# Five gated FFNs that multiply the unnormalized residual and take 1/rms at the read-out, in a two-block kernel on one core

## The chip, the cores and the metric

One core of a Trainium2 chip runs the whole program. The metric is the device time of one execution in microseconds, the median of several executions. TensorE multiplies, VectorE and ScalarE work elementwise, GpSimd adds a little, and 16 DMA engines bring the weights.

## What is computed

The reference runs two transformer blocks of two layers each on 256 tokens of width 1024. Cut to what matters here:

```python
def rmsnorm(x, gain):
    xf = x.astype(jnp.float32)
    y = xf * lax.rsqrt(jnp.mean(xf * xf, axis=-1, keepdims=True) + NORM_EPS)
    return (y * gain.astype(jnp.float32)).astype(x.dtype)

def modulate(h, shift, scale):
    return h * (1.0 + scale) + shift

def swiglu(u, wg, wu, wd):
    return (jax.nn.silu(u @ wg) * (u @ wu)) @ wd
...
    u = modulate(rmsnorm(h, norm_ffn2[l]), mod[:, :, 6], mod[:, :, 7])
    h = h + 0.5 * (1.0 + mod[:, :, 8]) * swiglu(u, ffn2_wg[l], ffn2_wu[l], ffn2_wd[l])
```

The first block has in each layer an FFN, a mixer (retention, stick-breaking attention, a state space part) and a second FFN; the second block has a mixer of three attentions and one FFN per layer. That is six FFNs with an inner width of 2816. The modulation vectors come from products of a condition vector with large matrices (the "ada" matrices).

## The kernel before

Everything is held transposed: width on the 128 partitions (8 tiles, KT), the 256 tokens along the free dimension. Stages follow in the order `STAGES`: f1, m1, f2 for each layer of the first block, a final norm, then m2, f3 for each layer of the second block (`FFN` numbers the six FFNs 0 to 5).

**Split products.** Every float32 product is made as three fp32r matmuls of high and low halves (`mm3`, lines 706 to 709): high weight by high and by low activation, low weight by high activation, each with its own weight load of 128x128 and 256 moving columns. All matmuls through the helper `mm` stand in the profile as L704.

**Weights.** One stream in the order of use: `fill`s of 1 MB by DMA from SP's queue into a ring of three slots, each two "grains" of 128x1024. ScalarE makes each grain's high half (`split`, L1246), VectorE its low half (L1728), into four slots; a slot is free when TensorE has read the grain four before.

**One FFN** (`ffn` in each engine's program). For each of the 22 inner tiles (a unit: one gate grain, one up grain) TensorE makes 2 x 8 x 3 matmuls into the two halves of one of four banks. Unit 0 goes by k, gate and up together, waiting for each k of u; the others go grain by grain. ScalarE takes the silu of the gate half from the bank (L1355), VectorE multiplies it by the up half (L1847), ScalarE copies the high half of the result (L1361), VectorE makes the low half (L1853). Then the down product: 8 output tiles of 22 x 3 matmuls, 22 grains; VectorE adds each to h (L1832), ScalarE squares it (L1336), GpSimd adds the squares (L2239).

**The norm in front of an FFN** (`norm`). The squares of h are summed over partitions by TensorE with a matrix of ones (`sums`: two float32 matmuls after an FFN, eight otherwise), then 18 matmuls into an unused bank (`idle`). ScalarE makes 1/rms by Ln and Exp (L1267, L1270). For each of the 8 tiles VectorE makes h * gain * 1/rms (L1749), ScalarE adds the shift and rounds to the high half of u (L1284), VectorE makes the low half (L1755). Before it, behind a mixer, VectorE adds the last product to h (`residual`, L1822) and ScalarE squares it (L1263).

**Ada turns.** The ada matrices stream through a ring of their own, one 128x1024 piece a turn: ScalarE issues the DMA (L1234), VectorE makes the dot product (L1703). `RATE_IN`, `RATE_OUT` and `RATE_MIX` are the turns per grain in gate/up, down and mixers; a stage that needs a vector takes all turns up to it first.

Of the kernel before, what the change touches and what calls it, by code (L numbers as in the profile page):

```python
# [14 lines left out]
F32 = mybir.dt.float32  # L15
# [7 lines left out]
P = 128  # L23
D = 1024
# [404 lines left out]
RATE_IN, RATE_OUT, RATE_MIX = 0.36, 0.48, 0.52  # L429
# [24 lines left out]
class Memory:  # L454


    def __init__(self, nc, ctx):
# [12 lines left out]
        self.rope_t = self.sb("rope_t", 2 * 512)  # L470
# [24 lines left out]
        self.o_low = [self.sb(f"o_low{i}", 2 * T, F32R, base + 4 * at) for i, at in enumerate(O_LOW_AT)]  # L495
        self.hid_split = self.sb("hid", 2 * FT * T, F32R, base + 4 * HID_AT)
        self.psum = ctx.enter_context(nc.psum_tensor("bank", [P, 8 * 512], F32))
        self.banks = [self.psum[:, i * 512:(i + 1) * 512] for i in range(8)]
        self.hv = tiles(self.h, KT)
# [152 lines left out]

def gate_of(s):
# [14 lines left out]
def after_ffn(s):  # L668

    n = STAGES.index(s)  # L670
    return n > 0 and STAGES[n - 1] in FFN

# [27 lines left out]
def pe_program(pe, m):  # L700
# [140 lines left out]

    def ffn(s):
# [3 lines left out]
        for n in range(TOGETHER if f == 0 else 0, FT):  # L846
# [380 lines left out]
def act_program(act, m, dram):  # L1227
# [26 lines left out]

    def norm(s):
        gain, scale, shift = norm_of(m, s)
        if not after_ffn(s):
# [7 lines left out]
        act.wait_ge(("square_read", s, KT - 1))  # L1265
        b = m.banks[act.bank("norm", s)]
        act.e.activation(m.rs[:, 0:T], b[:, 0:T], ACT.Ln, scale=1.0 / D, bias=m.eps[:, 0:1]) \  # L1267
            .then_inc(*act.done(("out", "norm", s), ("mean_log", s)))
        act.wait_ge(("mean_log", s))
        act.e.activation(m.rs[:, 0:T], m.rs[:, 0:T], ACT.Exp, scale=-0.5).then_inc(*act.done(("rs", s)))  # L1270
# [55 lines left out]

    def ffn(s):
# [4 lines left out]
        def square(d):  # L1332
            act.wait_ge(("h", s, d))
            if d >= 4:
                act.wait_ge(("square_sum", follows, d - 3))
            act.e.activation(m.squares[:, square_slot(d), :], m.hv[:, d, :], ACT.Square) \  # L1336
                .then_inc(*act.done(("square", follows, d)))
            if follows == STAGES[-1]:
# [6 lines left out]
        for t in range(FT + 1):  # L1345
# [3 lines left out]
            if together:  # L1349
                split(first + wanted_first(t))  # L1350
            if t:
# [343 lines left out]
def dve_program(dve, m):  # L1695
# [55 lines left out]

    def low_of(s, d, shift):
# [26 lines left out]
    def norm(s):  # L1779
        gain, scale, shift = norm_of(m, s)  # L1780
        for job in (scale, shift):
            if job:
                ada(dve.ada.until(job))
        if scale:
            dve.wait_ge(("params",), ("mod", JOB[scale]))
            last = STAGES[STAGES.index(s) - 1]
            dve.wait_ge(("gained", KT - 1) if last == STAGES[0] else ("scaled", last, KT - 1))
# [29 lines left out]
    def residual(s):  # L1817
        gate = gate_values(s)
        for d in range(KT):
# [4 lines left out]
                .then_inc(*dve.done(*points))  # L1824

    def ffn(s):
        f = FFN[s]
        first = STREAM.index[first_grain(s)]

        def add(d):  # L1830
# [3 lines left out]
                .then_inc(*dve.done(("h", s, d), ("out", "acc", s, d)))  # L1834

        split(first + 2)
        for t in range(FT + 1):
            n = t - 1
            g = m.inner[n % 2]
            together = f == 0 and t <= TOGETHER  # L1840
# [376 lines left out]
def pool_program(pool, m):  # L2217
# [13 lines left out]
    def squares(s):  # L2231

        pool.wait_ge(("square", s, 0))
        for d in range(1, KT - 1):
# [68 lines left out]
    for s in STAGES:  # L2303
        if after_ffn(s):
            squares(s)
# [239 lines left out]
```

## Time and profile before

| | us |
|---|---|
| median of 3 runs | 2032.94 (2025.23 to 2040.07) |
| the profiled execution | 2031.49 |
| its span | 2029.5 |
| TensorE busy | 1947.2 |
| VectorE busy | 1469.0 |
| ScalarE busy | 1041.2 |
| GpSimd busy | 140.3 |

The span runs from the first to the last instruction of the profiled execution, which took 2.0 us more. Busy times of different engines lie beside one another. The profile names PE (TensorE), PEld (its weight loads), DVE (VectorE), ACT (ScalarE), POOL (GpSimd) and SP (the queue that issues the weight stream).

### The profile page before, as it was taken

How to read it: one execution, taken by the hardware profiler on the slowest of the kernel's cores; microseconds unless marked ns; L12 is line 12 of the kernel's file. 1: busy time of each engine (PE TensorE's matmuls, PEld its weight loads, DVE VectorE, ACT ScalarE, POOL GpSimd, SP SyncE). 2: the span in 40 equal slices, each digit the busy share in tenths (PEclk: the TensorE clock that was granted, in tenths of full speed). 3: DMA queues.
4: the chain of work that ended last, by engine and by line, in shares of the span. 5: the costliest groups of instructions: out<-in, count | busy, mean ns of one | idle time of the engine just before them, and what ended most of it. 6: DMA issues, size and time to landing. Idle time of an engine off the chain costs nothing.

```text
span 2029.5 us, 38168 instructions
## 1 busy us (share of the span) xinstructions
PE 1947.2 (96%) x16020; PEld 1901.1 (94%) x16020; DVE 1469.0 (72%) x2244; ACT 1041.2 (51%) x1623; POOL 140.3 (7%) x130
## 2 busy tenths in 40 slices
PE   6999999999999999999999989998999899999998
PEld 6999899899999999999899989898999899989998
DVE  6777877776767777878766767778767778776553
ACT  4554655455545545564544455464554455545453
POOL 3100012100000000022000010001000100010000
PEclk9999999999999999999999999999999999999999
DMA  9678664567777785655577845466677655544552
GB/s 369 252 271 318 243 236 169 218 224 264 274 249 257 266 294 216 240 186 208 218 254 251 294 170 198 179 220 230 217 265 282 240 205 206 190 156 164 190 204 104
DMA packets 83835, 466.39 MB, mean 230 GB/s; under 512 B 9424, under 2 KB 9552, under 8 KB 44496
## 3 DMA queue, kind: packets, MB, share of 16 engines
q1 hardware_dynamic: 48544, 334.98, 45.6%
q10 hardware_dynamic: 35120, 128.99, 17.8%
q8 instruction: 125, 2.05, 0.4%
q14 instruction: 46, 0.38, 0.1%
HBM read 462.88 MB, written 1.05 MB: 229 GB/s over the span
## 4 chain that ended last, share of the span: by engine, by line
PE 72%; DVE 12%; ACT 4%; issue 2%; POOL 1%; DVEq 0%; ACTq 0%
PE bank L704 71%; DVE low L1728 4%; DVE ada_ring L1703 2%; ACT high L1246 1%; DVE tmp L1749 1%; DVE u_split L1755 1%; PE bank L1047 1%; DVE region L1887 0%; ACT u_split L1284 0%; DVE region L2133 0%; POOL region L2269 0%; DVE region L2184 0%; ACT rs L1267 0%; ACT rs L1270 0%; DVE region L1697 0%
## 5 line engine op out<-in xcount | busy, mean ns | idle before, releaser
L704 PE MATMUL bank<-u_split,high 128*128 128x256 f32 x6464 | 1137.5, 281 | 26.3 <-DVE u_split L1755 17.4
L704 PEld LDWEIGHTS bank<-u_split,high 128*128 128x128 f32 x6464 | 982.8, 188 | 37.9 <-DVE u_split L1755 18.9
L1728 DVE TENSOR_TENSOR low<-ring,high 128x1024 fp32r<-128x1024 f32 x616 | 751.2, 1233 | 355.7 <-issue 226.4
L704 PE MATMUL bank<-u_split,low 128*128 128x256 f32 x3232 | 899.2, 278 | 0.0
L1246 ACT ACTIVATE high<-ring 128x1024 fp32r<-128x1024 f32 x616 | 617.2, 1046 | 86.8 <-PE bank L704 78.3
L704 PEld LDWEIGHTS bank<-u_split,low 128*128 128x128 f32 x3232 | 607.5, 188 | 0.4
L704 PE MATMUL bank<-hid,high 128*128 128x256 f32 x2112 | 363.4, 277 | 0.7 <-DVE low L1728 0.7
L704 PEld LDWEIGHTS bank<-hid,high 128*128 128x128 f32 x2112 | 319.2, 188 | 0.9 <-DVE low L1728 0.9
L1703 DVE SCALAR_TENSOR_TENSOR ada_ring<-ada_ring,cond 128x1024 f32<-128x1024 f32 x242 | 300.5, 1242 | 2.8 <-DMA ada_ring<-ada 2.8
L704 PE MATMUL bank<-hid,low 128*128 128x256 f32 x1056 | 292.6, 277 | 0.0
L704 PEld LDWEIGHTS bank<-hid,low 128*128 128x128 f32 x1056 | 198.2, 188 | 0.0
L1355 ACT ACTIVATE sil<-bank 128x256 f32<-128x256 f32 x132 | 50.9, 385 | 232.3 <-PE bank L704 232.2
L1361 ACT ACTIVATE hid<-sil 128x256 fp32r<-128x256 f32 x132 | 55.3, 419 | 98.8 <-DVE sil L1847 98.8
L2239 POOL TENSOR_TENSOR tmp<-tmp 128x256 f32<-128x256 f32 x36 | 26.6, 739 | 1127.5 <-ACT tmp L1336 1127.5
L1336 ACT ACTIVATE tmp<-h 128x256 f32<-128x256 f32 x48 | 20.1, 418 | 145.7 <-DVE h L1832 145.7
L704 PE MATMUL bank<-region 128*128 128x256 f32 (+2 forms) x312 | 70.7, 352 | 6.4 <-DVE xa L1868 4.7
L704 PE MATMUL bank<-high,u_split 128*128 128x256 f32 (+1 forms) x384 | 68.4, 279 | 2.1 <-DVE low L1728 2.1
L704 PEld LDWEIGHTS bank<-region 128*128 128x128 f32 (+1 forms) x312 | 53.7, 190 | 15.6 <-DVE xa L1868 5.5
L1749 DVE SCALAR_TENSOR_TENSOR tmp<-h,gcol,rs 128x256 f32<-128x256 f32 x80 | 41.4, 534 | 31.9 <-ACT rs L1270 31.9
L704 PEld LDWEIGHTS bank<-high,u_split 128*128 128x128 f32 x384 | 58.9, 188 | 2.5 <-ACT region L1393 1.4
L1853 DVE TENSOR_TENSOR hid<-sil,hid 128x256 fp32r<-128x256 f32 x132 | 55.5, 420 | 6.8 <-ACT hid L1361 6.8
L704 PE MATMUL bank<-merged,high 128*128 128x256 f32 x256 | 48.0, 292 | 11.8 <-DVE merged L2188 8.3
(213 smaller groups left out, 1823.6 us busy)
## 6 DMA issues: line engine op xcount, KB each, us to landing
ring<-stream SPq DMA_DIRECT2D x302, 1024.0 KB, 5.5
ada_ring<-ada ACTq DMA_DIRECT2D x240, 512.0 KB, 4.2
region<-ada SPq DMA_DIRECT2D x6, 1024.0 KB, 12.7
ring<-stream SPq DMA_DIRECT2D x4, 640.0 KB, 4.4
region<-na_bias ACTq DMA_DIRECT2D x2, 1024.0 KB, 4.8
ring<-stream SPq DMA_DIRECT2D x4, 512.0 KB, 3.9
cst<-const SPq DMA_DIRECT2D x1, 1600.0 KB, 8.9
cond<-cond SPq DMA_DIRECT2D x2, 512.0 KB, 5.5
```

Of the source, the lines that this page charges most:

```text
L704: return pe.e.matmul(out, lhs, rhs, start=start, stop=stop, skip_group_check=True)
L1047: t = pe.e.transpose(b[:, k * T + a * P:k * T + (a + 1) * P], m.S[p][:, a * T + k * P:a * T + (k + 1) * P], m.c2("ident"))
L1246: act.e.activation(hi, src, ACT.Copy).then_inc(*act.done(("high", n)))
L1336: act.e.activation(m.squares[:, square_slot(d), :], m.hv[:, d, :], ACT.Square) \
L1355: act.e.activation(g, m.banks[act.bank("hid", f, n)][:, 0:T], ACT.Silu).then_inc(*act.done(("silu", f, n)))
L1361: act.e.activation(m.hid[0][:, n, :], g, ACT.Copy).then_inc(*act.done(("hid_high", f, n)))
L1703: dve.e.scalar_tensor_tensor(out=w, in0=w, scalar=1.0, in1=m.cond[:, block * D:(block + 1) * D], op0=ALU.mult, op1=ALU.mult, accum_out=m.s ...
L1728: dve.e.tensor_tensor(lo, src, hi.bitcast(F32), ALU.subtract).then_inc(*dve.done(("low", n)))
L1749: dve.e.scalar_tensor_tensor(out=out, in0=m.hv[:, d, :], scalar=gain[:, d:d + 1], in1=m.rs[:, 0:T], op0=ALU.mult, op1=ALU.mult).then_inc(* ...
L1755: dve.e.scalar_tensor_tensor(out=m.ul[:, d, :], in0=src, scalar=m.mod(shift)[:, d:d + 1], in1=m.uh[:, d, :].bitcast(F32), op0=ALU.add, op1 ...
L1853: dve.e.tensor_tensor(m.hid[1][:, n, :], g, m.hid[0][:, n, :].bitcast(F32), ALU.subtract) \
L2239: pool.e.tensor_tensor(total, total, m.squares[:, square_slot(d), :], ALU.add) \
```

## The change

The five FFNs 1 to 5 (all but the first) no longer build u. ScalarE and VectorE make v = h * gain * (1 + scale), split in two, in a tile of 320-column rows, with the shift in two more columns behind the 256 of h. TensorE multiplies 258 columns, gate and up into a bank each (`ffn_linear`), so columns 256 and 257 hold the shift's product. At the read-out VectorE multiplies both banks, 2 x 258 columns, by [1/rms, 1, 1] into `scaled_out`; ScalarE takes the silu with column 256 as its bias; VectorE adds the up half's column 256 and multiplies. The sum of the squares stands on TensorE between gate and up of unit 1, and ScalarE makes 1/rms (`root`) there. v is made inside the residual loop behind a mixer, and in the down stretch behind an FFN. GpSimd adds the squares at all five. The idle matmuls and the norm of these stages are gone. There are no ada turns in the first four units of these FFNs, and RATE_OUT is 0.64 for 0.48.

```diff
-RATE_IN, RATE_OUT, RATE_MIX = 0.36, 0.48, 0.52
+RATE_IN, RATE_OUT, RATE_MIX = 0.36, 0.64, 0.52
...
+LINEAR = [("f2", 0), ("f1", 1), ("f2", 1), ("f3", 0), ("f3", 1)]
+UNITS, UNITS_QUIET = FT, 4
+TE = T + 2
+V_AFTER = {3: (0, 1), 4: (2, 3), 5: (4, 5), 6: (6,)}
...
     def norm(s):
+        if s in LINEAR:
+            return
         sums(s)
         idle(s)
 
     def sums(s):
-        b = banks.take("work", "norm", s)
-        if after_ffn(s):
+        b = banks.open(7, "norm", s) if s in LINEAR else banks.take("work", "norm", s)
+        if pooled(s):
...
+    def ffn_linear(s):
+        f = FFN[s]
+        for n in range(UNITS):
+            bs = [banks.open((2 * n + i) % 8, "hid", f, n, i) for i in range(2)]
+            if n == 0:
+                gs = [grain("gate", f, n), grain("up", f, n)]
+                pe.wait_ge(("v_shift", s))
+                for k in range(KT):
+                    pe.wait_ge(("v", s, k))
+                    for i in range(2):
+                        t = mm3(bs[i][:, 0:TE], [x[:, k, :] for x in gs[i][1]], (m.vh[k], m.vl[k]), k == 0, k == KT - 1)
...
+                if n == 1 and i == 0:
+                    sums(s)
...
+    def v_high(s, d):
+        act.wait_ge(("gcol", s), before(s)[d])
+        act.e.activation(m.vh[d][:, 0:T], m.hv[:, d, :], ACT.Identity, scale=m.gcol[:, d:d + 1]) \
+            .then_inc(*act.done(("v_high", s, d)))
+    def prepare(s):
+        act.e.preload_act_table_set(LOG_EXP)
+        first = STREAM.index[first_grain(s)]
+        shift_columns(s)
+        for d in range(KT):
+            v_high(s, d)
+            if d >= 4:
+                act.wait_ge(("square_sum", s, d - 3))
+            act.e.activation(m.squares[:, square_slot(d), :], m.hv[:, d, :], ACT.Square).then_inc(*act.done(("square", s, d)))
+            if d == 5:
+                split(first + 3)
...
+        if t == 1:
+            root(s)
+        if t:
+            act.wait_ge(("scaled_out", f, n))
...
+            act.e.activation(g, m.scaled_out[n % 2][:, 0, 0:T], ACT.Silu, bias=m.scaled_out[n % 2][:, 0, T:T + 1]) \
+                .then_inc(*act.done(("silu", f, n)))
+        split(upto + 4)
...
+    def v_low(s, d):
+        dve.wait_ge(("v_high", s, d))
+        dve.e.scalar_tensor_tensor(out=m.vl[d][:, 0:T], in0=m.hv[:, d, :], scalar=m.gcol[:, d:d + 1],
+                                   in1=m.vh[d][:, 0:T].bitcast(F32), op0=ALU.mult, op1=ALU.subtract) \
+            .then_inc(*dve.done(("v", s, d)))
...
+                dve.wait_ge(("full", "hid", f, n), ("rs", s), ("rs_tail", s))
+                dve.e.tensor_tensor(m.scaled_out[n % 2], two(m.psum[:, i * 512:(i + 2) * 512])[:, :, 0:TE],
+                                    spread(m.rs[:, 0:TE], 2), ALU.mult) \
+                    .then_inc(*dve.done(("scaled_out", f, n), ("out", "hid", f, n, 0), ("out", "hid", f, n, 1)))
+                split(upto + 3)
+                dve.wait_ge(("silu", f, n))
+                dve.e.scalar_tensor_tensor(out=g, in0=m.scaled_out[n % 2][:, 1, 0:T], scalar=m.scaled_out[n % 2][:, 1, T:T + 1],
+                                           in1=g, op0=ALU.add, op1=ALU.mult).then_inc(*dve.done(("prod", f, n)))
+            split(upto + 4)
```

VectorE behind the first mixer, before: eight residuals (h), then the gain columns, then pairs of normalized tile (tmp) and low half (u_split).

```order
L1809 TENSOR_SCALAR gates<-mods 128x8
L1822 SCALAR_TENSOR_TENSOR h<-bank,gates,h 128x256 x8
L1788 SCALAR_TENSOR_TENSOR gcol<-mods,par 128x8
L1749 SCALAR_TENSOR_TENSOR tmp<-h,gcol,rs 128x256 x2
L1755 SCALAR_TENSOR_TENSOR u_split<-tmp,mods,u_split 128x256
```

The same place with the change:

```order
L1954 TENSOR_SCALAR gates<-mods 128x8
L1877 SCALAR_TENSOR_TENSOR gcol<-mods,par 128x8
L1970 SCALAR_TENSOR_TENSOR h<-bank,gates,h 128x256
L1884 TENSOR_TENSOR v<-mods,v 128x8x2
L1970 SCALAR_TENSOR_TENSOR h<-bank,gates,h 128x256
L1890 SCALAR_TENSOR_TENSOR v<-h,gcol,v 128x256
```

The low half of v now follows each residual, one tile behind; nothing of u is left.

VectorE in one later unit of the same FFN, before (low are weights, sil the product, hid the low half, ada_ring a turn):

```order
L1728 TENSOR_TENSOR low<-ring,high 128x1024
L1847 TENSOR_TENSOR sil<-sil,bank 128x256
L1728 TENSOR_TENSOR low<-ring,high 128x1024
L1853 TENSOR_TENSOR hid<-sil,hid 128x256
L1703 SCALAR_TENSOR_TENSOR ada_ring,sums<-ada_ring,cond 128x1024
```

and with the change:

```order
L2012 TENSOR_TENSOR rope_t<-bank,rs 128x516
L1846 TENSOR_TENSOR low<-ring,high 128x1024
L2017 SCALAR_TENSOR_TENSOR sil<-rope_t,sil 128x256
L1846 TENSOR_TENSOR low<-ring,high 128x1024
L2022 TENSOR_TENSOR hid<-sil,hid 128x256
L1821 SCALAR_TENSOR_TENSOR ada_ring,sums<-ada_ring,cond 128x1024
```

One pass out of the banks (rope_t is where `scaled_out` lies) stands ahead of the first weight split; the rest keeps its order.

## Rows read from the trace of the kernel before

**Rows 1.** The page: busy time by engine, share of the span, instructions.
```profile
PE 1947.2 (96%) x16020; PEld 1901.1 (94%) x16020; DVE 1469.0 (72%) x2244; ACT 1041.2 (51%) x1623; POOL 140.3 (7%) x130
```

**Rows 2.** The chain in order of time: start, length, engine, tile, line, count.
```profile
423.61 174.42 PE bank L704 x1536
```

**Rows 3.** Stretches: length, busy time (instructions) by engine, granted clock, DMA.
```profile
410.10:416.50 6.40, 5.88 (x36) 5.22 (x35) 3.81 (x11) 4.49 (x11) 0.00 (x0) 1.00 0.39 160
423.60:538.10 114.50, 114.50 (x1010) 114.50 (x1011) 83.07 (x118) 57.61 (x85) 0.00 (x0) 1.00 0.75 265
538.10:598.00 59.90, 59.90 (x530) 59.90 (x529) 41.87 (x55) 27.05 (x32) 4.42 (x6) 1.00 0.82 286
976.10:982.70 6.60, 3.73 (x23) 3.56 (x22) 6.57 (x10) 3.66 (x4) 0.00 (x0) 0.82 0.70 240
```

**Rows 4.** Timeline, TensorE: start, length, instruction, count [idle before, releaser].
```profile
410.12 3.70 PE L704 MATMUL bank<-tmp,ones 128*128 128x256 f32 x16
...
413.48 2.50 PE L704 MATMUL bank<-high 128*128 128x256 f32 x18
...
416.52 0.47 PE L704 MATMUL bank<-u_split,high 128*128 128x256 f32 x2 [0.54 <-DVE u_split L1755]
...
423.61 0.50 PE L704 MATMUL bank<-u_split,high 128*128 128x256 f32 x2 [0.74 <-DVE low L1728]
...
597.85 0.59 PE L704 MATMUL bank<-tmp,ones 128*128 128x256 f32 x2
...
609.51 0.51 PE L704 MATMUL bank<-u_split,high 128*128 128x256 f32 x2 [0.75 <-DVE low L1728]
...
999.86 0.50 PE L704 MATMUL bank<-u_split,high 128*128 128x256 f32 x2 [0.75 <-DVE low L1728]
...
1432.17 0.50 PE L704 MATMUL bank<-u_split,high 128*128 128x256 f32 x2 [0.74 <-DVE low L1728]
...
1845.70 0.50 PE L704 MATMUL bank<-u_split,high 128*128 128x256 f32 x2 [0.78 <-DVE low L1728]
```

**Rows 5.** Timeline: residuals on VectorE behind the four mixers; squares on ScalarE.
```profile
409.12 3.23 DVE L1822 SCALAR_TENSOR_TENSOR h<-bank,gates,h 128x256 f32<-128x256 f32 x8
...
409.63 3.16 ACT L1263 ACTIVATE tmp<-h 128x256 f32<-128x256 f32 x8 [2.38 <-DVE h L1822]
...
982.66 0.88 DVE L1822 SCALAR_TENSOR_TENSOR h<-bank,gates,h 128x256 f32<-128x256 f32 x2
...
1416.42 3.44 DVE L1822 SCALAR_TENSOR_TENSOR h<-bank,mods,h 128x256 f32<-128x256 f32 x8
...
1829.08 1.65 DVE L1822 SCALAR_TENSOR_TENSOR h<-bank,mods,h 128x256 f32<-128x256 f32 x4
```

**Rows 6.** Groups by form, VectorE and ScalarE: busy us, mean ns, idle before.
```profile
L1728 DVE TENSOR_TENSOR low<-ring,high 128x1024 fp32r<-128x1024 f32 x608 | 746.4, 1241 | 355.7 <-issue 226.4 <-ACT high L1246 128.2
...
L1755 DVE SCALAR_TENSOR_TENSOR u_split<-tmp,mods,u_split 128x256 fp32r<-128x256 f32 x72 | 34.6, 481 | 3.3 <-ACT u_split L1284 3.3
...
L1697 DVE COPY region<-bank 128x512 f32<-128x512 f32 x10 | 6.9, 687 | 1.5 <-PE bank L704 1.5
...
L1246 ACT ACTIVATE high<-ring 128x1024 fp32r<-128x1024 f32 x608 | 613.1, 1052 | 86.8 <-PE bank L704 78.3 <-DVE ada_ring L1703 6.9 <-DMA ring<-stream 1.1
...
L1318 ACT ACTIVATE full<-h,gcol 128x256 f32<-128x256 f32 x8 | 4.0, 505 | 0.2
```

**Rows 7.** Timeline, VectorE, one unit of the second layer's first FFN.
```profile
643.90 1.22 DVE L1728 TENSOR_TENSOR low<-ring,high 128x1024 fp32r<-128x1024 f32 x1 [1.27 <-issue]
...
646.84 1.22 DVE L1703 SCALAR_TENSOR_TENSOR ada_ring<-ada_ring,cond 128x1024 f32<-128x1024 f32 x1
...
649.34 1.23 DVE L1728 TENSOR_TENSOR low<-ring,high 128x1024 fp32r<-128x1024 f32 x1 [1.27 <-issue]
```

**Rows 8.** Timeline, TensorE: products with 128 moving columns.
```profile
1255.28 0.39 PE L704 MATMUL bank<-high,u_split 128*128 128x128 f32 x2
...
1259.64 0.39 PE L704 MATMUL bank<-high,u_split 128*128 128x128 f32 x2
```

More of the change, by code:

```diff
@@ L498, in __init__ @@
         self.banks = [self.psum[:, i * 512:(i + 1) * 512] for i in range(8)]
+        self.scaled_out = [two(self.rope_t[:, i * 520:i * 520 + 2 * TE]) for i in range(2)]
         self.hv = tiles(self.h, KT)
@@ L840, in ffn_first @@
                         t.then_inc(*pe.done(*points))
+    def ffn_linear(s):
[9 more added lines that the diff above has]
+                        t = mm3(bs[i][:, 0:TE], [x[:, k, :] for x in gs[i][1]], (m.vh[k], m.vl[k]), k == 0, k == KT - 1)
+                t.then_inc(*pe.done(("read", gs[0][0]), ("read", gs[1][0]), ("full", "hid", f, n)))
+                continue
+            for i, what in enumerate(("gate", "up")):
+                r, g = grain(what, f, n)
+                for k in range(KT):
+                    t = mm3(bs[i][:, 0:TE], [x[:, k, :] for x in g], (m.vh[k], m.vl[k]), k == 0, k == KT - 1)
+                t.then_inc(*pe.done(("read", r), *([("full", "hid", f, n)] if i else [])))
+                if n == 1 and i == 0:
+                    sums(s)
     def ffn(s):
@@ L845, in ffn @@
             ffn_first(s)
-        for n in range(TOGETHER if f == 0 else 0, FT):
+        if s in LINEAR:
+            ffn_linear(s)
+        for n in range(TOGETHER if f == 0 else UNITS if s in LINEAR else 0, FT):
             b = banks.take("work", "hid", f, n)
@@ L1253, in grains, with shift_columns, root @@
             ada(act.ada.turns(rate_of(key)))
+    def shift_columns(s):
+        _, scale, shift = norm_of(m, s)
+        for job in (scale, shift):
+            ada(act.ada.until(job))
+        act.wait_ge(("mod", JOB[shift]), ("sum", STAGES[STAGES.index(s) - 1], 0))
+        act.e.activation(m.v_shift[0], m.mod(shift).unsqueeze(2).broadcast_to([P, KT, 2]), ACT.Copy) \
+            .then_inc(*act.done(("shift_high", s)))
+    def v_high(s, d):
[13 more added lines that the diff above has]
+                split(first + 3)
+    def root(s):
+        act.wait_ge(("square_read", s, KT - 1))
+        b = m.banks[act.bank("norm", s)]
+        act.e.activation(m.rs[:, 0:T], b[:, 0:T], ACT.Ln, scale=1.0 / D, bias=m.eps[:, 0:1]) \
+            .then_inc(*act.done(("out", "norm", s), ("mean_log", s)))
+        act.wait_ge(("mean_log", s))
+        act.e.activation(m.rs[:, 0:T], m.rs[:, 0:T], ACT.Exp, scale=-0.5).then_inc(*act.done(("rs", s)))
     def norm(s):
         gain, scale, shift = norm_of(m, s)
+        if s in LINEAR:
+            if not after_ffn(s):
+                prepare(s)
+            return
         if not after_ffn(s):
@@ L1350, in ffn @@
                 split(first + wanted_first(t))
+            if s in LINEAR and t <= UNITS:
+                linear(s, f, first, t)
+                continue
             if t:
@@ L1750, in scaled, with gain_columns, shift_columns @@
                                    op0=ALU.mult, op1=ALU.mult).then_inc(*dve.done(*points))
+    def gain_columns(s):
+        gain, scale, shift = norm_of(m, s)
+        last = STAGES[STAGES.index(s) - 1]
+        for job in (scale, shift):
+            ada(dve.ada.until(job))
+        dve.wait_ge(("params",), ("mod", JOB[scale]), ("v", last, KT - 1) if last in LINEAR else ("scaled", last, KT - 1))
+        dve.e.scalar_tensor_tensor(out=m.gcol[:, :], in0=m.mod(scale), scalar=1.0, in1=gain, op0=ALU.add, op1=ALU.mult) \
+            .then_inc(*dve.done(("gcol", s)))
+        dve.wait_ge(("gcol", s))
+    def shift_columns(s):
+        dve.wait_ge(("shift_high", s))
+        dve.e.tensor_tensor(m.v_shift[1], m.mod(norm_of(m, s)[2]).unsqueeze(2).broadcast_to([P, KT, 2]),
+                            m.v_shift[0].bitcast(F32), ALU.subtract).then_inc(*dve.done(("v_shift", s)))
+    def v_low(s, d):
[3 more added lines that the diff above has]
+            .then_inc(*dve.done(("v", s, d)))
     def low_of(s, d, shift):
@@ L1824, in residual @@
                 .then_inc(*dve.done(*points))
+            if follows in LINEAR:
+                if d == 0:
+                    shift_columns(follows)
+                else:
+                    v_low(follows, d - 1)
+        if follows in LINEAR:
+            v_low(follows, KT - 1)
     def ffn(s):
```

79 lines of the change are left out of this document (70 added, 9 removed).

## The prediction

> **What bounds the kernel now.** I read the busy shares first, then the chain that ended last in order of time, then the stretches around one FFN, and last the timeline of the five places where an FFN in question begins. TensorE is busy for 96% of the span [rows 1]; inside an FFN it never waits: 1536 matmuls stand in one piece of 174.42 us, 113.5 ns each [rows 2]. VectorE is busy for 83.07 of 114.50 us in a gate/up stretch and ScalarE for 57.61 [rows 3], so there both have room. What can still be saved is the seam in front of each FFN. "Unit n" is inner tile n, with its gate and its up (48 matmuls, 5.44 us at 113.3 ns).
>
> The seam after the first mixer reads so [rows 4]: the mixer's last output matmuls go until 410.12, then come 8 float32 matmuls that sum the squares (16 records, to 413.48, so 0.42 us each), 18 matmuls on nothing until 1/rms and the first split of u are there, unit 0 from 416.52, paced by the splits of u, and unit 1 not before 423.61. It waits for a low half of the weights, because VectorE made eight pairs of u first. From the last useful matmul to unit 1 that is 13.5 us for 5.44 us of work. The four seams behind a mixer all have this form; the one between two FFNs goes from 597.85 to 609.51, 11.7 us.
>
> **The change, part by part.** (a) Unit 0 no longer waits for 1/rms, only for v = gain*h split in two. Behind a mixer, v is made inside the residual loop: per tile d VectorE issues the residual and the low half, ScalarE the high half and the square. VectorE's eight residuals took 3.23 us and ScalarE's eight squares 3.16 us [rows 5], 0.40 us each, so both engines need about 0.81 us per d; with the handovers I take 0.85. ScalarE also splits one grain after d = 5, another 1.05 us [rows 6]. From the first residual h0: 0.30 for gcol and shift columns, 0.48 to its result, 7 x 0.85 = 5.95, 1.05 for the grain, 0.51 for the last high half, 0.48 for the last low half, and the low half of unit 1's gate grain, 1.24 [rows 6]: h0 + 10.0. That is when unit 1 can start. Unit 0 is hidden in it if the mixer's last matmul + 5.44 comes earlier, which holds at all four seams. Bounds: h0 + 9.0 (pipelined handovers) and h0 + 13.5 (1.3 us per d, each handover in full). With h0 at 409.12, 982.66, 1416.42 and 1829.08 [rows 5] and unit 1 before at 423.61, 999.86, 1432.17 and 1845.70 [rows 4], the four seams give 4.5 + 7.2 + 5.8 + 6.6 = 24.1 us (28.1 and 10.1 at the bounds).
>
> (b) Between the two FFNs, v0 to v6 are made while the last output tile is still being multiplied, so unit 0 starts at once at 597.85. v7 needs residual, high half and low half, 0.48 + 0.51 + 0.48 plus handovers, ready near 599.6, long before unit 0 wants it (42 matmuls, 4.8 us). Unit 1 starts at 603.3 instead of 609.51: 6.2 us (5.0 if the low half of unit 1's grain is late). The work that hides these splits is the down stretch, where VectorE is busy for only 41.87 of 59.90 us [rows 3]; it gets 8 low halves and 4 more ada turns there (14 for 10), about 9 us, and stays below the stretch.
>
> (c) The sum of squares moves into unit 1, where TensorE has no bubble: two float32 matmuls at 0.42 us, 0.85 us x 5 = 4.3 us lost. Behind a mixer the additions of the squares go to GpSimd; it has until the middle of unit 1. The 18 empty matmuls go, all of them bubble: nothing.
>
> (d) 258 columns instead of 256 in 5 x 22 x 2 x 8 x 3 = 5280 matmuls. No row has 258. Both sides: if columns set the pace, 113.3/256 = 0.44 ns a column, 0.885 ns per matmul, 4.7 us. If something else does, nothing. The nearest row speaks for the second: with 128 moving columns, 13 triples go by from 1255.28 to 1259.64, 111.8 ns per matmul [rows 8], against 113.3 for 256. I take 1.0 us. In the Trainium skill, "TensorE: Matmul & The Clock Gate", section "Back-to-back issue gap", the isolated gap grows with N/2.4 ns and the real pace is set by weight load and matmul together. By its first formula alone 5280 x 0.83 would be 4.4 us, an estimate; the trace's pace at 128 columns, 111.8 ns, agrees with the second half of that section, not with the formula.
>
> (e) The read-out of a unit gets longer. VectorE before: a period of 5.44 us from 643.90 to 649.34 with an ada turn, of which 1.27 idle, so 4.17 of work [rows 7]. It gains one pass over both banks, 516 elements; a 512-wide pass out of the banks is 687 ns [rows 6]; the product stays one pass. So 4.2 + 0.7 = 4.9 us of 5.44, and 3.7 in a unit without ada turn. While ScalarE takes the silu, VectorE has a low half to make, and another one while ScalarE makes the high half of the hidden tile: both handovers are covered by 1.1 us of work against about 0.5. Four slots of weights and four pairs of banks let VectorE lag by some 2 us before TensorE stands. Cost 0; the bound above is the third rival. Unit 0's read-out waits for 1/rms, some 3.7 us behind unit 1's start, and for a table load, and runs late until unit 2 or 3; that delay too stays under the 5.44 us that each next unit covers.
>
> (f) Ada turns: none in the first four units, more in the down stretch, total the same; three mixers hold one turn less (27, 30 and 22 for 28, 31 and 23, counted in VectorE's order). VectorE is in the mixers' chain, so 0 to 3.7 us, taken 1.0.
>
> Sum: -24.1 - 6.2 + 4.3 + 1.0 + 0 - 1.0 = -26.0 us. The profiled execution took 2031.5 us (span 2029.5 and 2.0 around it), which gives 2005.5; the median of the three runs is 1.4 us above the profiled one. I forecast 2006 us, own range 1998 to 2014 (all good bounds together reach -33.7, 1998; columns at full price and one microsecond more at each seam reach 2014). A measurement here tells about 1% (20 us) from no change.
>
> **Rivals.** First: the new chain of v takes the place of the old wait. For: VectorE and ScalarE hand each tile to and fro, residual, high, low, and the wait of each is behind the other's next operation. Against: 0.40 us per operation in rows that alternate less. Price: h0 + 13.5, 14 us given back, 2019.5, within 1%.
>
> Second: TensorE's clock. The empty matmuls go, and the granted clock, 1.00 in the seam stretch from 410.1, was 0.82 from 976.1 to 982.7, where TensorE was busy for only 3.73 of 6.60 us [rows 3]: part of that at 1.2 instead of 2.4 GHz. If it falls at each mixer seam and one unit goes by at half rate, 4 x 5.4 = 22 us come back: 2027, within 1%. Against: the longest new gap is about 1 us (410.1 until the first v at about 411), and then 6 matmuls per 0.85 us are 0.69 us of work. In the Trainium skill the same page (Part 1) says that the default is the half clock and that dense work releases it; idle matmuls are then worth their place, and these five seams lose them. So far the trace bears out the fall at a stall, and no row shows one at so small a gap.
>
> Third, the slower side: the read-out becomes the bound. Place: scaled_out, silu, product, high, low of every unit. If VectorE sees both ScalarE handovers in full (0.5 us each) and the high half of the up grain late (0.1 to 0.3), its period is 4.7 + 1.3 = 6.0 us, 0.57 over TensorE's, in about 105 units: +60 us, 2065. It decides against the change from a period of 5.68 us (26/105 = 0.25 above 5.44). Against: each handover has a covering operation, and the mean need is 4.7.
>
> **How the numbers follow.** Forecast 0.76, first rival 0.11, second 0.08, third 0.05. The forecast's range reaches past the 1% line (2011) with a tenth of its share: faster 0.69, within 1% 0.26, slower 0.05. Leaving out the third rival and part of the second, the range is 1998 to 2022.
>
> **What would show it.** In the profile of the changed kernel: unit 1 starting 10 us behind the first residual of each mixer seam, and 5.5 us behind the last matmul between the two FFNs; no 18 matmuls except at the unchanged stages; 258-column stretches at 113.5 ns per matmul (114.2 if columns count); VectorE at about 97 of 114.5 us in gate/up, with TensorE never waiting there; granted clock 1.00 in the seams. Wrong would be: TensorE waiting for low halves in units 2 to 21, unit 1 later than h0 + 11, or a clock under 1.00 in unit 0.

## The result and the profile after

| | before | after |
|---|---|---|
| median, us | 2034.89 (2025.23 to 2041.62, 15 runs) | 2043.40 (2039.48 to 2050.06, 15 runs) |
| the profiled execution, us | 2031.49 | 2050.06 |
| its span | 2029.5 | 2048.3 |

The ratio of after to before is 1.0053, with a 95% interval of 1.0037 to 1.0070. The change makes the kernel 0.5% slower: the interval lies above 1, but the difference is under the 1% that the prediction called the least it could tell from no change. The forecast was 2006 us, with a range of 1998 to 2022, so the time lies outside the range. The profiled execution of after happens to be the slowest of its 15; a second profile (after_again) stands below.

The page and the groups of after, by form (busy us, mean ns of one, idle before):

```profile
PE 1967.5 (96%) x15882; PEld 1922.6 (94%) x15882; DVE 1539.0 (75%) x2319; ACT 1060.3 (52%) x1628; POOL 159.2 (8%) x159
...
L1846 DVE TENSOR_TENSOR low<-ring,high 128x1024 fp32r<-128x1024 f32 x608 | 744.2, 1236 | 166.8 <-ACT high L1294 111.2 <-issue 54.7
...
L726 PE MATMUL bank<-v,high 128*128 128x258 f32 x3520 | 642.0, 285 | 3.0 <-DVE v L1890 1.5 <-DVE low L1846 1.3
...
L2012 DVE TENSOR_TENSOR rope_t<-bank,rs 128x516 f32<-128x516 f32 x110 | 76.4, 695 | 142.0 <-PE bank L726 134.8 <-ACT rs L1338 7.1
...
L726 PE MATMUL bank<-hid,high 128*128 128x256 f32 x2112 | 367.1, 279 | 3.3 <-DVE low L1846 3.3
```

Against [rows 1] TensorE has 138 records less and is busy for 20.3 us more: fewer matmuls (at each mixer seam 12 records for the sums and 18 on nothing, between the two FFNs 18), and longer ones with 258 columns. The 258-column group waits for v and for low halves for only 3.0 us in 3520 matmuls, so it is not a wait that ate the gain. VectorE's new pass over both banks is 695 ns (0.7 was taken).

The seams came as the prediction said. TensorE's timeline of after, behind the first mixer and between the two FFNs (start, length, instruction, count, idle before and its releaser):

```profile
418.62 0.48 PE L726 MATMUL bank<-v,high 128*128 128x258 f32 x2 [0.78 <-DVE v L1890]
...
426.30 0.48 PE L726 MATMUL bank<-v,high 128*128 128x258 f32 x2 [0.23 <-DVE low L1846]
...
609.65 0.28 PE L726 MATMUL bank<-hid,low 128*128 128x256 f32 x1
...
610.88 0.48 PE L726 MATMUL bank<-v,high 128*128 128x258 f32 x2 [0.95 <-DVE low L1846]
```

and VectorE's, the first and the last tile of v in the same seam:

```profile
416.87 0.48 DVE L1970 SCALAR_TENSOR_TENSOR h<-bank,gates,h 128x256 f32<-128x256 f32 x1
...
417.99 0.48 DVE L1890 SCALAR_TENSOR_TENSOR v<-h,gcol,v 128x256 fp32r<-128x256 f32 x1 [0.16 <-ACT v L1315]
...
424.36 0.66 DVE L1890 SCALAR_TENSOR_TENSOR v<-h,gcol,v 128x256 fp32r<-128x256 f32 x1 [0.22 <-ACT v L1315]
```

The first residual (h0) starts at 416.87 and unit 1 at 426.30, which is h0 + 9.4; it was h0 + 14.5 in [rows 4, 5], and h0 + 10.0 was forecast. Between the two FFNs unit 0 starts 0.95 us behind the last matmul on hid.

What is not as forecast is what follows a seam. The chain in order of time, after (start, length, engine, tile, line, records):

```profile
610.88 128.73 PE bank L726 x1060
...
1140.26 54.71 PE bank L726 x480
...
1438.75 122.98 PE bank L726 x1012
...
1567.72 56.82 PE bank L726 x480
```

A piece with 1012 records is units 1 to 21 of an FFN, 21 x 48 = 1008 matmuls of 258 columns, and the four records of the sum of squares (two float32 matmuls, 0.85 us); the one with 1060 has unit 0 too, and one with 480 is a down product (528 matmuls) without its first 48. (122.98 - 0.85) / 1008 = 121.2 ns a matmul, where [rows 2] gives 113.5. From the starts of ScalarE's silus the period of a unit, 48 matmuls, is 5.80 us (120.8 ns a matmul; the piece also has the edges of its first and last matmul) in all five FFNs, and was 5.44 us (113.3 ns). That is 7.5 ns a matmul, and x 5280 it is 39.6 us. The granted clock is not the cause (stretch of after: length, busy by engine as in [rows 3], then the granted clock):

```profile
424.60:540.00 115.40, 115.17 (x949) 114.79 (x949) 89.94 (x126) 61.41 (x85) 0.13 (x1) 1.00 0.67 233
```

It is 1.00, so 2.4 GHz. At that clock 5.44 us a unit are 272 cycles a matmul and 5.80 us are 290. Figures "by the unit" below are always such a period between silus divided by 48.

### The profile page after: what moved, and what is told of

It is laid out like the page before. It is cut to its first block, busy times and chain, and to the rows that moved or that the text cites. A ratio compares the mean times of both kernels' runs of the same rounds, so it can differ in the third digit from the quotient of the medians.

```text
span 2048.3 us, 38015 instructions
## 1 busy us (share of the span) xinstructions
PE 1967.5 (96%) x15882; PEld 1922.6 (94%) x15882; DVE 1539.0 (75%) x2319; ACT 1060.3 (52%) x1628; POOL 159.2 (8%) x159
## 4 chain that ended last, share of the span: by engine, by line
PE 58%; DVE 8%; ACT 4%; issue 2%; POOL 0%; ACTq 0%; DVEq 0%
PE bank L726 57%; DVE low L1846 3%; ACT high L1294 1%; DVE ada_ring L1821 1%; PE bank L1095 1%; DVE u_split L1897 0%; DVE region L2328 0%; DVE region L2379 0%; DVE tmp L1867 0%; DVE region L2082 0%; DVE v L1890 0%; DVE h L1970 0%; ACT v L1315 0%; DVE h L1989 0%; ACT h L1365 0%
## 5 line engine op out<-in xcount | busy, mean ns | idle before, releaser
L1294 ACT ACTIVATE high<-ring 128x1024 fp32r<-128x1024 f32 x616 | 626.6, 1045 | 114.2 <-PE bank L726 95.7
L726 PE MATMUL bank<-v,high 128*128 128x258 f32 x3520 | 642.0, 285 | 3.0 <-DVE v L1890 1.5
L726 PEld LDWEIGHTS bank<-v,high 128*128 128x128 f32 x3520 | 549.0, 191 | 5.7 <-DVE v L1890 2.1
L726 PE MATMUL bank<-u_split,high 128*128 128x256 f32 (+2 forms) x2944 | 531.5, 285 | 20.2 <-DVE u_split L1897 14.6
L726 PE MATMUL bank<-v,low 128*128 128x258 f32 x1760 | 499.8, 284 | 0.0
L726 PEld LDWEIGHTS bank<-u_split,high 128*128 128x128 f32 (+2 forms) x2944 | 452.0, 189 | 29.1 <-DVE u_split L1897 15.2
L726 PE MATMUL bank<-u_split,low 128*128 128x256 f32 (+1 forms) x1472 | 412.6, 280 | 0.0
L726 PEld LDWEIGHTS bank<-v,low 128*128 128x128 f32 x1760 | 336.2, 191 | 0.0
L726 PEld LDWEIGHTS bank<-u_split,low 128*128 128x128 f32 (+1 forms) x1472 | 278.0, 189 | 0.5
L1425 ACT ACTIVATE sil<-rope_t 128x256 f32<-128x256 f32 x110 | 56.3, 512 | 253.8 <-DVE rope_t L2012 253.0
L2012 DVE TENSOR_TENSOR rope_t<-bank,rs 128x516 f32<-128x516 f32 x110 | 76.4, 695 | 142.0 <-PE bank L726 134.8
```

What stands on the lines that cost most here:

```text
L726: return pe.e.matmul(out, lhs, rhs, start=start, stop=stop, skip_group_check=True)
L1294: act.e.activation(hi, src, ACT.Copy).then_inc(*act.done(("high", n)))
L1425: act.e.activation(g, m.scaled_out[n % 2][:, 0, 0:T], ACT.Silu, bias=m.scaled_out[n % 2][:, 0, T:T + 1]) \
L2012: dve.e.tensor_tensor(m.scaled_out[n % 2], two(m.psum[:, i * 512:(i + 2) * 512])[:, :, 0:TE], spread(m.rs[:, 0:TE], 2), ALU.mult) \
```

## The experiments

The theory after the result: two more moving columns lengthen each matmul by a step of some 7 ns. The rivals: the second bank that gate and up now have, the layout of v, the longer read-out, or this one execution.

**The change without the two columns.** w256 multiplies 256 columns on TensorE in place of 258; the layout of v, the banks and the seams stay, and so does the read-out pass, with 512 elements for 516. The shift's product is left out and a constant takes its place in the read-out. w260 and w320 go the other way, with the shift's product in place.

```diff
+TM = 256
-t = mm3(bs[i][:, 0:TE], ..., (m.vh[k], m.vl[k]), k == 0, k == KT - 1)
+t = mm3(bs[i][:, 0:TM], ..., (m.vh[k], m.vl[k]), k == 0, k == KT - 1)
```

(TM = 260 and 320 in the two others; the rows of v hold TM columns, those past 256 filled with the shift.)

> The changed kernel with 256 moving columns in the five FFNs' gate and up products in place of 258: the shift's product is left out, and the read-out uses a constant in its place; everything else, the layout of v, the two banks per unit and the read-out, stays. Theory A (any width over 256 columns costs a fixed 8 ns per matmul; the profile after shows 121.5 ns where 256 columns show 113.4): 5280 x 8.1 ns = 43 us go, the time is about 2001 us, and the pace in gate/up is 113.4 ns. Theory B (the slower pace comes from the layout of v or from the two banks per unit): the pace stays at 121 ns and the time near 2043.

> The changed kernel with 260 moving columns (the shift in four columns, two of them unused). Theory A1 (a fixed step above 256): pace 121.5 to 122.3 ns, time within 5 us of the changed kernel's 2043. Theory A2 (each column above 256 costs about 4 ns): pace 129.5 ns, 43 us more, about 2086.

> The changed kernel with 320 moving columns. A1 (a fixed step, then the plain column rate of 0.42 ns): pace 121.5 + 62 x 0.42 = 147 ns, time about 2043 + 137 = 2180. If the plain column rate alone held from 256 on, without a step: 113.4 + 26.7 = 140 ns. A2: over 350 ns.

> The kernel before, once more, for its profile. In the profile of the changed kernel the first FFN, which the change leaves alone, takes 5.65 us per unit (117.7 ns per matmul) where the profile of the kernel before has 5.44 (113.3). Theory S (executions differ in this): units of the first FFN anywhere from 5.44 to 5.65 us, and if 5.65, a time near 2041. Theory T (the moved buffers of the changed kernel do it): 5.44 us here and 5.65 in the three runs beside it.

w256 took 2005.04 us (2002.09 to 2007.16, 4 runs) beside 2036.43 of the kernel before: ratio 0.9851 (0.9819 to 0.9883). w260 took 2038.62 us, w320 2181.25 us, the kernel before, profiled again, 2030.52 us. The chains of w256, w260 and w320, units 1 to 21 of one FFN each:

```profile
1407.88 115.43 PE bank L727 x1012
```
```profile
1428.30 122.10 PE bank L727 x1012
```
```profile
420.92 148.96 PE bank L727 x1012
```

By the unit that is 113.3, 120.0 and 146.7 ns. The two columns alone are worth 2043.40 - 2005.04 = 38.4 us, 39.6 by the count of matmuls. The second bank, the layout of v and the pass over both banks stand in w256 too, and its units run at 5.44 us: within a unit they cost nothing (behind the last unit the pass does, see (e) below). And 260 columns are no dearer than 258, so it is no price by the column: there is a step behind 256. For w320 the step and 0.42 ns a column had been expected to give 147 ns and 2180 us, and did.

**The same kernels once more.** The profiled execution of after was its slowest, so here is another.

> The changed kernel once more, for a second profile. So far: 258 columns at 5.80 us per unit (120.8 ns per matmul) in all five FFNs, but in an execution whose unchanged first FFN also ran slow, at 5.65. Theory A (the columns make it): 5.76 to 5.80 again although the first FFN is at 5.44; time about 2041. Theory S (a slow execution made part of it): 5.56 us, as in the six wide units of hyb6; time about 2022.

It took 2038.06 us, span 2036.3, and its units again 5.80 us in all five FFNs, as by theory A. (The 5.56 us that this expectation took from hyb6 are ScalarE's silus while the read-out catches up; TensorE's own wide units there are 5.80 us too, as hyb6 below shows.) The 12.0 us between the two profiled spans lie elsewhere: 2.8 us up to the end of FFN 0's gate/up stretch, which the change doesn't touch and which ran its units at 5.65 us in the first and 5.44 in the second, 5.0 us in down products, at 56.8 or 54.7 us per 480 matmuls (both stand in the chain above), and the rest nearly all in the mixers. The kernel before has these two paces too. In both of its profiles FFN 3 runs at the slower one throughout, gate/up and down:

```profile
999.86 181.19 PE bank L704 x1536
```

(chain of before, FFN 3: 118.0 ns a matmul, against 113.5 in [rows 2].) FFN 0 of before_again ended at 5.44 us a unit, as in the three runs beside it, so that run alone decides between neither theory; that it differs between after and after_again, the same kernel, speaks for S. So the spans of two executions can differ by more than the change does, and what a change is worth must be read stage by stage.

**What the step hangs on: width.**

```diff
-TM = 256
-t = mm3(bs[i][:, 0:TM], ..., (m.vh[k], m.vl[k]), k == 0, k == KT - 1)
+TN, OFF = 252, 0
+t = mm3(bs[i][:, 0:TN], ..., (m.vh[k][:, OFF:OFF + TN], m.vl[k][:, OFF:OFF + TN]), k == 0, k == KT - 1)
```

(w252; TN is 240 in w240 and 248 in w248, and the last 4, 16 or 8 tokens are left out, as is the shift's product; w272 is w260 with TM = 272.)

> The kernel of w256 with only 252 moving columns (the last four tokens are left out of gate and up). Theory A (a step above 256): pace at or below w256's 113.7 ns. Theory A3 (256 is the special width, and every other width pays about 4.8 ns over 0.444 ns a column, the line through 260 and 320): 4.8 + 111.9 = 116.7 ns, slower than 256 although narrower. Time about 2003 by A, 2020 by A3.

> The changed kernel with 272 moving columns. Theory G (the moving row is taken in pieces of 16 columns, 64 bytes, so that 258, 260 and 272 columns cost the same 17 pieces): 5.76 us per unit, time near w260's 2038. Theory L (a fixed cost and 0.444 ns a column, the line through 260 and 320): 125.6 ns, 6.03 us per unit, about 2066.

> 240 moving columns from the row's start (16 tokens and the shift's product are left out). If the pace is the larger of a floor set by the weight load and the columns plus a constant, 240 is on the floor: 111.8 to 113.3 ns a matmul, units of 5.37 to 5.44 us, 2000 to 2005. If any count but 256 is dear, as 252 seemed to say, units take 5.6 us or more: 2020 or over.

> 248 moving columns from the row's start (8 tokens and the shift's product are left out). If the floor holds up to 256, units take 5.38 to 5.44 us: 1996 to 2005. If the count must be a multiple of 16, as 252 hints, units take 5.6 us or more in some FFNs: 2015 or over.

| columns | us | ns a matmul by the unit, FFNs 1 to 5 |
|---|---|---|
| 240 | 1996.35 | 112.1 in all |
| 248 | 2019.42 | 116.7, 116.7, 113.3, 113.3, 116.7 |
| 252 | 2027.23 | 120.0, 113.3, 116.7, 116.7, 120.0 |
| 256 | 2005.04 | 113.3 in all |
| 258 | 2038.06 | 120.8 in all |
| 260 | 2038.62 | 120.0 in all |
| 272 | 2057.23 | 123.3 in all but one (126.7) |
| 320 | 2181.25 | 146.7 in all |

(One profiled execution each, w256's time from four; 258 is after_again.) The chains of w240, w272 and w248, the last with two FFNs:

```profile
1403.63 114.04 PE bank L728 x1012
```
```profile
1443.38 125.48 PE bank L727 x1012
```
```profile
1418.09 115.45 PE bank L728 x1012
...
1828.87 118.67 PE bank L728 x1012
```

With [rows 8] (111.8 ns at 128 columns) and 240 columns at 112.1 there is a floor near 112 ns. Above 256 the time rises, from 272 to 320 by 23.4 / 48 = 0.49 ns a column, or by 0.42, one cycle, from the one FFN of w272 that ran at 126.7. Of the expectations the floor at 240 held. 272 columns cost neither what 258 and 260 do (G) nor the 125.6 ns of the line (L). Neither theory for 252 and 248 fits either: both widths run at different paces in different FFNs of one execution, the cheapest at 113.3 as with 256 columns, and each of the five FFNs keeps its pace from its third unit to its last.

**What the step hangs on: where the row starts.** 256 columns, read from column 2, 16, 32 or 64 of the rows of v (the shift's product is left out and the tokens stand that many columns off); step264 instead sets the rows 264 columns apart.

```diff
-TN, OFF = 252, 0
+TN, OFF = 256, 2
```

(16, 32 and 64 in the others; step264 is w256 with V_STEP = 264 for 320.)

> The kernel of w256 with its 256 columns read from column 2 of each row of v on, written to column 0 of the bank (the tokens are shifted by two, the shift columns fall in). If the number of columns makes the cost, the pace stays at 113.7 ns and the time near 2003; if the read of a row that is not on its 1280-byte start or runs past column 256 makes it, the pace is that of 258, 121 ns, and the time near 2043.

> As off2, with the 256 columns read from column 16 on, a multiple of 64 bytes. Theory G: 16 whole pieces, 5.44 us per unit as in w256, about 2003 us. If the start of the row itself matters: 5.76 as in off2, about 2036.

> 256 moving columns as in w256, read from column 64 of each row of v (256 bytes behind its start; the shift's product is left out and the tokens stand 64 columns off). If a start inside the row is what costs, whatever the distance, units take 5.76 us as with an offset of 2 and 16 columns, and the time is 2038. If only starts that are not a multiple of 256 bytes from the row's start cost, units take 5.44 us and the time is 2005.

> w256 with rows of v 264 columns apart instead of 320, so that only every second row starts on a multiple of 64 bytes (1056 bytes a row); 256 moving columns from each row's start, the shift's product left out. If the start's alignment to 64 bytes decides, about half of the matmuls take 120 ns and units take 5.6 us: 2022. If the first column of a row is cheap wherever it lies, units take 5.44 us: 2005.

> 256 moving columns read from column 32 of each row of v, 128 bytes behind its start (the shift's product is left out, the tokens stand 32 columns off). If a row must touch no more than eight pieces of 128 bytes, units take 5.44 us and the time is 2005 to 2011. If the pieces are 256 bytes, units take 5.76 us and the time is 2038.

| start of the row, bytes | us | ns a matmul by the unit, FFNs 1 to 5 |
|---|---|---|
| 0 (w256) | 2005.04 | 113.3 in all |
| 8 (off2) | 2037.83 | 120.0 in all but one (121.7) |
| 64 (off16) | 2038.45 | 120.0 in all |
| 128 (off32) | 2029.02 | 117.7 in all |
| 256 (off64) | 2010.78 | 113.3 in all but one (117.7) |
| 0 to 224, in steps of 32 (step264) | 2032.36 | 118.3 in all |

The chains of off2, off32 and off64:

```profile
1429.64 122.09 PE bank L728 x1012
```
```profile
1424.11 119.86 PE bank L728 x1012
```
```profile
1823.51 115.42 PE bank L728 x1012
```

The same 256 columns cost 120.0 ns from 8 or 64 bytes inside the row, as much as 258 or 260 columns from the start, and 113.3 ns from the row's start or 256 bytes on. So the number of columns alone does not decide; where the moving row begins or ends does too. Start and end move together in these runs, and none separates them. The reading that fits most of them is that a row of exactly 1024 bytes from such a start stays within some blocks, and that any shift or excess touches one more; but 128 bytes gave 117.7, neither the 113.3 of blocks of 128 bytes nor the 120.0 of blocks of 256, and 252 columns stay within the row of 256 and are dearer all the same. Besides, 117.7 is also the second pace of unshifted 256 columns (FFN 3 of before, one FFN of off64), so off32, one execution, may show that pace in all five FFNs and not a price of its start. step264, whose rows start at eight different places, lies between with 118.3. The reading is argued, not shown.

**Fewer wide matmuls.** Of the three matmuls of a product only high by high takes 258 columns in hihi; the low terms of the shift are left out, and all else is the changed kernel.

```diff
+def mm3w(out, lhs, rhs, first, final):
+    mm(out, lhs[0], rhs[0], first, False)
+    mm(out[:, 0:T], lhs[0], rhs[1][:, 0:T], False, False)
+    return mm(out[:, 0:T], lhs[1], rhs[0][:, 0:T], False, final)
```

> The changed kernel with 258 columns in the first of the three matmuls of each product (high by high) and 256 in the other two; the two low terms of the shift's product are left out. If each matmul over 256 pays for itself, a third of the cost stays: 1760 x 7.5 = 13 us, about 2018 us, mean pace 116.2 ns. If the whole accumulation group pays once it is wide, near 2043.

> The kernel with 258 columns only in the high by high matmul and 256 in the two others (the low terms of the shift left out), timed in five rounds. From its single profile (units of 5.65 us, 2028.2): 2029, ratio 0.995 to the kernel before, faster. If its single profile was a fortunate execution: 2036, ratio 1.0.

Its profiled execution took 2028.24 us, units of 5.65 us in all FFNs (117.7 ns). The cost isn't the wide matmul's alone: over ten units of FFN 1 the second matmul starts 117.2 ns behind the first (the wide one), the third 119.5 behind the second and the next first 116.7 behind the third, where w256 has 113, 113 and 114. So mixing saves less than two thirds: of 0.36 us a unit, 0.15 are back, and neither theory (2018 or 2043) came true. Timed, it is at 2030.29 us (2028.57 to 2034.41, 12 runs) beside 2033.15 (17 runs): ratio 0.9984, interval 0.9968 to 1.0001, which includes 1. The version kept the 2029 of its expectation, but not the 0.995: that gain was that of a kernel before at 2037.51 in the batch of its first execution.

**Fewer wide units.** The changed form only in the first units, u made meanwhile and 256 columns with the old read-out after them. In hyb6 units 0 to 5 are wide, in hyb5 units 0 to 4.

```diff
-UNITS, UNITS_QUIET = FT, 4
+UNITS, UNITS_QUIET = 6, 6
+U_AT = {2: (0, 1), 3: (2, 3), 4: (4, 5), 5: (6, 7)}
-RATE_IN, RATE_OUT, RATE_MIX = 0.36, 0.64, 0.52
+RATE_IN, RATE_OUT, RATE_MIX = 0.36, 0.70, 0.52
...
+if s in LINEAR and n == UNITS and i == 0:
+    pe.wait_ge(("u", s, k))
```

(hyb5: 5 and 5, three tiles of u a unit, rate 0.66.)

> A version meant to keep the seams and drop the columns: units 0 to 5 of the five FFNs as in the changed kernel, units 6 to 21 with u and 256 columns as before; u is made in the read-outs of units 1 to 4, two tiles in each, ada turns rest until unit 6 and RATE_OUT is 0.70. Columns: 5 x 6 x 48 x 7.5 ns = 10.8 us instead of 39.6; everything else as in w256 (2005). Expected 2015 us, ratio to before 0.990. If the splits of u make VectorE late, TensorE waits for u or low halves in units 4 to 8, up to 2 us in each of the five FFNs, about 2025.

> As hyb6 with five wide units instead of six, u made in three read-outs instead of four, and ada turns closer to the changed kernel's (quiet until unit 5, RATE_OUT 0.66), so that the down stretch of the first of the five FFNs isn't late by 4.5 us as in hyb6. In hyb6 the 256-column units of two FFNs ran at 5.65 us instead of 5.44, as those of one FFN do in the kernel before. If that is drawn anew at each FFN, the time is 2015 to 2035 with a median about 2024, ratio 0.994; if u makes TensorE wait, over 2030.

hyb6 took 2034.15 us (2027.56 to 2046.77, 10 runs) beside 2037.51: 0.9989 (0.9963 to 1.0014). hyb5 took 2035.68 (2029.60 to 2045.15, 10 runs) beside 2031.03: 1.0028 (1.0003 to 1.0053). Neither reached the 2015 and 2024 of its expectation. In both profiles the mixer seams keep their gain (unit 1 at h0 + 9.3 to 9.4; h0 is the first residual) and TensorE's wide units take 5.80 us. In hyb6 the wide units 1 to 5 cost 5 x 5 x 0.36 = 9 us against w256, the 256-column units ran at 5.65 us in FFNs 1 and 2 and 5.44 in the three others (16 x 0.21 x 2 = 6.7 us), and from FFN 1's first down matmul to the next unit 0 it took 65.8 us for 61.8 in w256, with the ada turns pushed into it. In hyb5 TensorE stands behind unit 4 (TensorE's timeline, then the stretch that follows, with the granted clock):

```profile
446.58 0.51 PE L727 MATMUL bank<-u_split,high 128*128 128x256 f32 x2 [2.27 <-DVE rope_t L2018]
```
```profile
448.10:451.60 3.50, 3.50 (x19) 3.50 (x18) 1.52 (x2) 0.42 (x1) 0.00 (x0) 0.53 0.26 80
```

That is 2.26 to 2.28 us in each of the five FFNs: VectorE makes u in units that already have the extra pass. And in four of the five the granted clock falls a moment later, here to 0.53 of 2.4 GHz, so most of the stretch at 1.2: the matmuls stand 213 ns apart, and unit 5 takes 7.2 to 7.3 us for 5.44 or 5.65. With the idle time that is some 19 us, the over 2030 us of the expectation. No version that computes everything beat the kernel before; w256 did, without the shift.

## Why the prediction was wrong, point by point

- **(a), four mixer seams, -24.1: right.** Unit 1 was forecast at h0 + 10.0; it came at h0 + 9.43, 9.35 and 9.34 in the three seams of after whose unit 1 has a row of its own, and w256 gives 9.43, 9.34, 9.35 and 9.35. Against 14.49, 17.20, 15.75 and 16.62 in [rows 4, 5] w256 gained 64.06 - 37.47 = 26.6 us. The handovers of v cost what was taken: VectorE's residuals stand 0.88 us apart in the middle, for 0.85.
- **(b), the seam between FFNs, -6.2: 5.1 in w256, near the 5.0 of the worse case.** Unit 0 waited 0.91 us for a low half of its weights, because VectorE had a v to make first; the prediction had thought of unit 1's grain, and of 5.0. TensorE's timeline of w256, the first mixer seam's unit 1, then this seam:

```profile
419.97 0.47 PE L727 MATMUL bank<-v,high 128*128 128x256 f32 x2 [0.28 <-DVE low L1847]
...
595.80 0.28 PE L727 MATMUL bank<-hid,low 128*128 128x256 f32 x1
...
596.98 0.47 PE L727 MATMUL bank<-v,high 128*128 128x256 f32 x2 [0.91 <-DVE low L1847]
```

  Unit 1, 48 matmuls on, is at 602.51, 6.71 us behind the start of the last matmul on hid (595.80). In before it was 609.51 - 597.73 = 11.78.
- **(c), the sums, +4.3: right,** 4.2 us: from unit 1 to the first down matmul w256 takes 0.76 to 0.89 us more than before in the four FFNs that have the same pace in both.
- **(e), the read-out, 0: right for the units, 4.3 us short behind the last one.** Units take 5.44 us in w256 with the full pass, and VectorE is busy for 89.9 of 115.4 us in after's stretch above, less than the forecast's 97. The third rival (6.0 us a unit) was 0.2 us from looking like the result, 5.80 us, but w256 excludes it. What the prediction left out is the end of the gate/up stretch, where no later unit covers the read-out: ScalarE splits the down product's weights only behind the last hidden tile and a table load, and that is now later, by the new pass and what it hands on to ScalarE. ScalarE's timeline of before and of w256, then TensorE's of w256 at the second grain:

```profile
540.78 3.91 ACT L1246 ACTIVATE high<-ring 128x1024 fp32r<-128x1024 f32 x4
```
```profile
538.91 2.95 ACT L1295 ACTIVATE high<-ring 128x1024 fp32r<-128x1024 f32 x3
...
541.38 0.50 PE L727 MATMUL bank<-hid,high 128*128 128x256 f32 x2 [0.59 <-DVE low L1847]
```

  The split starts 2.8 us behind the first down matmul in before (537.98) and 3.7 in w256 (535.19). TensorE then waits, in all five FFNs of w256 and after; in before gate/up and down stand in one unbroken piece [rows 2], and none of the five waits there. The down product takes 0.86 us more for it, 4.3 us in all.
- **(f), ada turns, -1.0: right in size, its cause not shown.** The four mixer stretches, from the last residual of an FFN to the first of the next seam, sum to 0.9 us less in w256 than in before (2.0 in after_again). But the first two are longer (by 0.7 and 1.5) and the last two shorter (by 1.1 and 2.0), and how much of it is the turns isn't shown.
- **(d), 258 columns, +1.0 of 0 to 4.7: this step failed.** It measured 39.6 us by the periods, 38.4 by the medians, and 37.9 by the pieces of after_again against w256, because behind a mixer unit 0's matmuls hide behind v. The prediction bounded it above by "113.3/256 = 0.44 ns a column", as though the time per column that a 256-wide matmul shows on average were the most that two more can cost. The row with 128 columns at nearly the same time had said that the pace is a floor, and a floor tells nothing of what stands behind its end; I took it for the nearest row and read it as "columns don't count". Two columns cost 7.5 ns, 3.7 ns each, eight times the bound; why the step is there stays open. It is the one term that is multiplied by 5280.

The sum without (d) was -27.0. w256's span is 28.0 us under that of before (2001.5 for 2029.5), and its pieces say from where:

| piece | us against before |
|---|---|
| four mixer seams | -26.6 |
| seam between FFNs | -5.1 |
| sums of squares | +4.2 |
| late splits in front of the down products | +4.3 |
| mixers | -0.9 |
| up to FFN 0's first down matmul | +0.7 |
| pace: FFN 3 gate/up -4.4, FFN 3 down -2.3, FFN 4 down +2.1 | -4.6 |

Without the pace that is -23.4. That it comes within 4 us of the -27.0 is in part luck, because errors cancel: the mixer seams gained 2.5 us more than forecast, and the late splits cost 4.3 that the sum didn't have. With (d) at 37.9 it makes +14.5. after_again's span is 6.8 us over that of before: the same pieces, less the 6.7 us that FFN 3 lost at the slower pace in before and not here, and 1.1 in the mixers. The medians say +8.5. Whether the change or chance took FFN 3 off the slower pace is open; 258-column units have shown only one.

**The rivals.** The chain of v at h0 + 13.5: not seen (9.4). The clock: 1.00 from 417.5 to 426.3, nearly the whole seam, with the 18 matmuls on nothing gone; where the idle time grew to 2.3 us, in hyb5, it did fall. It is 0.91 from 985.0 to 1003.0, where TensorE idles 3.25 of 18 us, but there an idle of 2.66 us stands in the mixer ahead of its last products, as in [rows 3], not in the seam. The read-out: no. The forecast's check "114.2 if columns count" was the right place to look; the row says 121.

## What to carry to other kernels

A pace that is the same at 128 and 256 columns is a floor; before widening past the last width that the trace shows, price the step as unknown and multiply it by the count of matmuls, since a term that applies thousands of times deserves the wide bound and not the nearest row. If an extra column has to go somewhere, it does not belong in the moving row of every matmul of a kernel whose TensorE is busy for 96%: five seams that give 32 us together, less 8.5 for the sums and the late splits, do not pay for 5280 steps of 7.5 ns. The order of the seam itself (v instead of u, 1/rms at the read-out) is worth 23 us here for whoever can add the shift at 256 columns; that wasn't found in these runs. And a pass that later units cover must be priced again behind the last unit, where nothing covers it.

## What the runs showed of the hardware

- fp32r matmuls each with a 128x128 weight load, at a granted clock of 1.00: 112.1 ns at 240 moving columns, 113.3 at 256, 120.0 to 120.8 at 258 and 260, 123.3 at 272, 146.7 at 320. In the Trainium skill, "TensorE: Matmul & The Clock Gate", section "Back-to-back issue gap", the isolated gap is N/2.4 + 2.5 ns; worked out from it, an estimate by that page, that is 109.2, 110.0, 110.8, 115.8 and 135.8 for 256, 258, 260, 272 and 320 columns. The measurement decides: the runs lie 4 ns over it at 256 and 7 to 11 ns over it beyond, and the formula has no step. That the real pace is set by weight load and matmul together, as the section says, is in keeping with the floor near 112 ns, but no run here changes the weight load, and the section's measured figure for 128 columns is about 81 ns, where this kernel takes 111.8 [rows 8].
- Where a moving row lies counts: 256 columns took 120.0 ns from 8 or 64 bytes inside the row of v, 117.7 from 128, 113.3 from 0 or 256.
- The same code with 256 columns has two paces, 113.3 and 117.7 ns (54.7 and 56.8 us for 480 matmuls of a down product), at a granted clock of 1.00. FFNs 1 to 5 keep theirs through a gate/up stretch, but it isn't tied to a stage: FFN 0 of before runs units 8 and 9 at 5.65 us by TensorE's starts and, behind two waits (0.46 and 0.14 us), units 13 to 20 at 5.44. It differs from execution to execution: FFN 0 at 5.44 or 5.65 us a unit in the two profiles of after. The kernel before ranges over 16 us in its 15 runs, and the other pace is worth 2 us in a down stretch and 4.4 in a gate/up stretch (21 units of 0.21). What picks the pace is open, as is why 248 and 252 columns have a pace for each FFN.
- TensorE idle for 2.27 us in a dense stretch (hyb5, in front of unit 5): the granted clock fell from 2.4 to 1.2 GHz in four of five such places, and stayed up in the fifth (1872 us). The matmuls then stood 213 ns apart.
